# Leaving out fifteen unread products ahead of three norms in a two-model kernel

## The chip, the cores and the metric

The kernel runs on one core of one Trainium2 chip, as one launch. The metric is the device time of that launch in microseconds (us). The engines are TensorE (PE, with its weight loads shown apart as PEld), VectorE (DVE), ScalarE (ACT), GpSimd (POOL) and SyncE (SP), which issues the DMAs.

## The reference

Two small models run one after the other on a sequence of 256 tokens of width 1024, batch 1, all in float32. The first has a recurrent layer and an attention layer, each with a gated feed-forward part. The second has two hybrid layers; each projects a normed residual stream into several mixers, merges their outputs, and adds a normed result to the residual, twice:

```python
h = rmsnorm_2(h_res, n_mix_pre)
proj = jnp.einsum('bld,de->ble', h, w_in)
...
mix = jnp.einsum('bld,de->ble', merged, w_out)
h_res = h_res + rmsnorm_2(mix, n_mix_post)
f = jnp.einsum('bld,df->blf', rmsnorm_2(h_res, n_ffn_pre), w_ffn_in)
f_gate, f_up = jnp.split(f, 2, axis=-1)
f = jnp.einsum('blf,fd->bld', jax.nn.silu(f_gate) * f_up, w_ffn_out)
return h_res + rmsnorm_2(f, n_ffn_post)
```

The norm ahead of an addition to the residual (`n_mix_post`, `n_ffn_post`) needs the mean square over all 1024 features, and the next projection needs the new residual. That is the place the change touches: between `w_out` and `w_ffn_in` of both layers, and between `w_ffn_out` of layer 0 and `w_in` of layer 1.

## The kernel before

The work is a list of phases (`plan()`), and a phase is a list of weight chunks of 128 output features by up to 1024 inputs. Tokens lie along the free dimension (256, or 272 with 16 meta tokens), features along the 128 partitions. SP loads a chunk into one of eight slots; ACT rounds it to a high part, DVE subtracts to get the low part, and PE makes three products for each block of 128 inputs (`three`): high by high, high by low, low by high. Each engine has its program written out by hand in order, and engines meet at semaphores.

The three places are the starts of the phases `ffn_up2`, `a_cx1` and `ffn_up3`. The order there is:

1. The last chunk of the phase before (`mix_out0`, `ffn_down2`, `mix_out1`) ends. PE adds up the squares over the partitions with a product by a matrix of ones (`sum_up`, lines 676 and 681), into the PSUM bank `B[0]`.
2. PE runs `keep_busy(5)`: five products of ones by a piece of the parameter table, into the bank `B[3]` (line 691). No instruction reads what they write, and they wait for no semaphore.
3. ACT makes the inverse root of the sum (lines 1246 and 1247), DVE scales the first tile of the mixed output and adds it to the residual (lines 1841 and 1843), and ACT scales that tile into the high part of the next right-hand side (line 1214). The other seven tiles follow (`new_x`), with their low parts made by DVE (line 1740).
4. PE begins the phase with four chunks at once (`raw_group`), block by block: at block k it waits for the high part of tile k, makes two products for each of the four chunks (`high_two`, lines 526 and 527), waits for the low part of tile k, and makes the third product (`low_one`, line 531).

The other norms of the second kind (`ffn0`, `kv`, `ffn1`, `pre0`) have no such products. At the very end, behind the last norm, there are none either: `last_x` adds the last tiles with six useful products (lines 947 and 950).

Of the kernel before, what the change touches and what calls it, by code (L numbers as in the profile page):

```python
# [237 lines left out]
def two_layer_pair(nc, a, out):  # L238
# [4 lines left out]
    with ctx:  # L243
# [271 lines left out]
        def _(pe):  # L515
# [168 lines left out]
                last.then_inc(sum_done, 1)  # L684


            IDLE = {"ffn_up2": 5, "a_cx1": 5, "ffn_up3": 5}

            def keep_busy(n):
                for _ in range(n):  # L690
                    pe.matmul(B[3][:, 0:SEQ], ONES[:, :], PV[:, 0:SEQ], start=True, stop=True)
# [214 lines left out]
            def run(name, ready=None, beside=None, inside=None, last_turn=None):  # L906
                p = by[name]
                seen = [0, 0]
                keep_busy(IDLE.get(name, 0))
                for i, xs in enumerate(p.groups()):  # L910
# [1484 lines left out]
```

## Time and profile before

| | us |
|---|---|
| median of 3 runs | 2192.72 (2192.27 to 2192.75) |
| the profiled execution, its own time | 2192.19 |
| its span, first to last instruction | 2190.4 |
| TensorE busy in the span | 2179.9 |
| VectorE busy | 1539.2 |
| ScalarE busy | 1163.9 |
| mean granted TensorE clock | 1.000 of full speed |

An engine's busy time is the union of its instructions' times; for TensorE the ends are modelled, so that matmuls overlap in the rows and the distance of their starts says more than one row's duration. A plain float32 product appears as two matmul rows.

### The profile page before, as it was taken

The page shows a single profiled execution, that of the slowest core. Times are in us where ns is not written, and L with a number is a line of the kernel's source. Part 1 is how long each engine was busy: PE and PEld are TensorE (multiplying, and loading weights), DVE is VectorE, ACT ScalarE, POOL GpSimd, SP SyncE. Part 2 cuts the span into 40 slices and gives each one's busy share as a digit, 9 for nine tenths or more (in the row PEclk, how much of TensorE's full clock was granted, in tenths as well). Part 3 has the DMA queues.
Part 4 walks back from the last instruction along what each step waited for, and adds up shares of the span by engine and source line. Part 5 has one row for each costly group of instructions (what it writes and reads, how often), then busy time and mean ns, then how long its engine had stood idle before and what let it go on. Part 6 is the DMA issues. An engine that isn't in the chain of part 4 may idle for free.

```text
span 2190.4 us, 40748 instructions
## 1 busy us (share of the span) xinstructions
PE 2179.9 (100%) x17034; PEld 2123.9 (97%) x17034; DVE 1539.2 (70%) x2568; ACT 1163.9 (53%) x1948; POOL 2.1 (0%) x6
## 2 busy tenths in 40 slices
PE   9999999999999999999999999999999999999999
PEld 7899999999999999999999999999999999999998
DVE  7878987776577679746655765596979556667663
ACT  3644545554544667446644644454766456546443
POOL 0000000000000000000000000000000000000000
PEclk9999999999999999999999999999999999999999
DMA  8879995367655654544355555565654544455653
GB/s 348 328 256 376 391 368 211 129 237 223 183 182 170 195 170 145 163 135 145 120 168 173 159 175 168 156 200 181 199 166 145 178 127 130 155 182 175 187 177 116
DMA packets 122984, 426.75 MB, mean 195 GB/s; under 512 B 14449, under 2 KB 18993, under 8 KB 122162
## 3 DMA queue, kind: packets, MB, share of 16 engines
q1 hardware_dynamic: 122802, 424.14, 58.8%
q8 instruction: 136, 2.23, 0.4%
q14 instruction: 46, 0.38, 0.0%
HBM read 421.43 MB, written 2.66 MB: 194 GB/s over the span
## 4 chain that ended last, share of the span: by engine, by line
PE 94%; DVE 3%; ACT 2%; issue 0%; DMA 0%; ACTq 0%
PE stream L519 26%; PE stream L521 26%; PE stream L520 26%; PE stream L535 6%; PE side L741 2%; PE side L748 1%; DVE w_lo L431 1%; PE side L535 1%; PE side L670 1%; PE side L882 0%; PE stream L526 0%; PE stream L527 0%; PE stream L531 0%; PE side L531 0%; PE side L527 0%
## 5 line engine op out<-in xcount | busy, mean ns | idle before, releaser
L519 PE MATMUL stream<-h_hi,w_hi 128*128 128x272 f32 (+1 forms) x3264 | 940.6, 288 | 0.7 <-DVE h_lo L1817 0.5
L521 PE MATMUL stream<-h_hi,w_lo 128*128 128x272 f32 (+1 forms) x3264 | 931.2, 285 | 0.0
L520 PE MATMUL stream<-h_lo,w_hi 128*128 128x272 f32 (+1 forms) x3264 | 929.1, 285 | 0.0
L431 DVE TENSOR_TENSOR w_lo<-raw,w_hi 128x1024 fp32r<-128x1024 f32 (+1 forms) x640 | 766.8, 1205 | 147.4 <-ACT w_hi L1038 146.1
L1038 ACT CAST w_hi<-raw 128x1024 fp32r<-128x1024 f32 (+1 forms) x640 | 652.4, 1035 | 249.6 <-DMA raw<-in_ffn_down 87.6
L519 PEld LDWEIGHTS stream<-h_hi,w_hi 128*128 128x128 f32 x3264 | 615.5, 189 | 4.8 <-DVE h_lo L1817 1.6
L521 PEld LDWEIGHTS stream<-h_hi,w_lo 128*128 128x128 f32 x3264 | 615.7, 189 | 0.0
L520 PEld LDWEIGHTS stream<-h_lo,w_hi 128*128 128x128 f32 x3264 | 614.4, 188 | 0.5
L519 PE MATMUL stream<-f_hi,w_hi 128*128 128x256 f32 (+1 forms) x704 | 198.9, 283 | 0.0
L521 PE MATMUL stream<-f_hi,w_lo 128*128 128x256 f32 (+1 forms) x704 | 198.6, 282 | 0.0
L520 PE MATMUL stream<-f_lo,w_hi 128*128 128x256 f32 (+1 forms) x704 | 198.1, 281 | 0.0
L520 PEld LDWEIGHTS stream<-f_lo,w_hi 128*128 128x128 f32 x704 | 133.1, 189 | 0.0
L521 PEld LDWEIGHTS stream<-f_hi,w_lo 128*128 128x128 f32 x704 | 132.4, 188 | 0.0
L519 PEld LDWEIGHTS stream<-f_hi,w_hi 128*128 128x128 f32 x704 | 132.1, 188 | 0.0
L1551 DVE SCALAR_TENSOR_TENSOR mod_raw<-mod_raw,silu_c 128x1024 f32<-128x1024 f32 x96 | 116.2, 1217 | 7.5 <-DMA mod_raw<-in_mod_w 7.5
L1629 DVE TENSOR_TENSOR conv_out<-conv_in,stream 128x256 f32<-128x256 f32 (+1 forms) x88 | 37.2, 422 | 119.4 <-PE stream L521 119.4
L1146 ACT ACTIVATE conv_in<-stream 128x256 f32<-128x256 f32 (+1 forms) x104 | 40.3, 388 | 130.6 <-PE stream L521 130.6
L1758 DVE TENSOR_TENSOR conv_out<-stream,rstd 128x272 f32<-128x272 f32 (+2 forms) x104 | 44.5, 430 | 71.9 <-PE stream L521 69.1
L519 PE MATMUL stream<-y_hi,w_hi 128*128 128x256 f32 (+1 forms) x320 | 91.6, 286 | 0.0
L521 PE MATMUL stream<-y_hi,w_lo 128*128 128x256 f32 (+1 forms) x320 | 90.7, 284 | 0.0
L520 PE MATMUL stream<-y_lo,w_hi 128*128 128x256 f32 (+1 forms) x320 | 90.7, 283 | 0.0
L535 PE MATMUL stream<-h_raw,raw 128*128 128x256 f32 (+1 forms) x384 | 85.6, 380 | 0.0
(409 smaller groups left out, 3064.2 us busy)
## 6 DMA issues: line engine op xcount, KB each, us to landing
raw<-in_ffn_up SPq DMA_DIRECT2D x176, 512.0 KB, 3.6
mod_raw<-in_mod_w SPq DMA_DIRECT2D x96, 512.0 KB, 5.9
raw<-in_ffn_down SPq DMA_DIRECT2D x64, 512.0 KB, 3.7
raw<-in_a_cx SPq DMA_DIRECT2D x32, 512.0 KB, 3.9
raw<-in_up_a SPq DMA_DIRECT2D x32, 512.0 KB, 3.5
raw<-in_up_b SPq DMA_DIRECT2D x32, 512.0 KB, 3.5
raw<-in_b_kq SPq DMA_DIRECT2D x32, 512.0 KB, 3.5
raw<-in_up_c SPq DMA_DIRECT2D x32, 512.0 KB, 3.5
```

The costliest lines, as they stand in the source:

```text
L431: eng.tensor_tensor(w_lo[:, x.slot, 0:x.kb * P], raw[:, x.slot, 0:x.kb * P], w_hi[:, x.slot, 0:x.kb * P].bitcast(F32), ALU.subtract).then_ ...
L519: pe.matmul(ps, w_hi[:, x.slot, W], rhs[0][:, k, off:off + n], start=first, stop=False)
L520: pe.matmul(ps, w_hi[:, x.slot, W], rhs[1][:, k, off:off + n], start=False, stop=False)
L521: return pe.matmul(ps, w_lo[:, x.slot, W], rhs[0][:, k, off:off + n], start=False, stop=last)
L535: return pe.matmul(ps, raw[:, x.slot, wcol * P:(wcol + 1) * P], rhs[0][:, k, off:off + n], start=first, stop=last)
L670: last = pe.transpose(b[0:n, i * P:(i + 1) * P], CO[:, p.slot[t], q:q + n], ident)
L741: last = pe.matmul(b[0:m, c:c + w], key[:, at:at + m], q[:, TOK * (qt + i) + q0:TOK * (qt + i) + q0 + w], start=i == 0, stop=i == tiles - 1)
L1038: act.copy(w_hi[:, x.slot, 0:x.kb * P], raw[:, x.slot, 0:x.kb * P]).then_inc(hi_ready, 1)
L1146: act.activation(CI[:, c, 3:3 + p.T], bank[s][:, 0:p.T], func).then_inc(bank_free[s], 1)
L1551: stt(w, w, 1.0, CBC[:, :], ALU.mult, ALU.mult, accum_out=MACC[:, m:m + 1]).then_inc(mod_done, 1)
L1629: tt(dst, f, bank[s][:, 0:T], ALU.mult).then_inc(bank_free[s], 1)
L1758: tt(dst, ps, root, ALU.mult).then_inc(bank_free[s], 1)
```

## The change

The table that says how many unread products stand ahead of a phase is emptied, so that `keep_busy` issues none. Nothing else is changed: the waits, the banks, the order and the other engines' programs stay.

```diff
--- before.py
+++ after.py
@@ -684,7 +684,7 @@
                 last.then_inc(sum_done, 1)
 
 
-            IDLE = {"ffn_up2": 5, "a_cx1": 5, "ffn_up3": 5}
+            IDLE = {}
 
             def keep_busy(n):
                 for _ in range(n):
```

## Rows read from the trace of the kernel before

**Rows 1.** The page: busy time, share of the span and instructions of each engine.

```profile
PE 2179.9 (100%) x17034; PEld 2123.9 (97%) x17034; DVE 1539.2 (70%) x2568; ACT 1163.9 (53%) x1948; POOL 2.1 (0%) x6
```

**Rows 2.** The chain in order of time around the first place: start, us, piece.

```profile
1208.23 0.74 PE side L681 x2
...
1208.99 0.49 ACT rstd L1246
...
1209.51 0.44 ACT rstd L1247
...
1209.97 0.45 DVE scratch L1841
...
1210.45 0.45 DVE x_res L1843
...
1210.93 0.53 ACT h_hi L1214
...
1211.50 0.39 PE stream L526
```

**Rows 3.** TensorE's timeline at `ffn_up2`: start, us, instruction [idle before <-releaser].

```profile
1208.23 0.73 PE L681 MATMUL side<-scratch,ones 128*128 128x272 f32 x2
1208.79 2.32 PE L691 MATMUL side<-params,ones 128*128 128x256 f32 x10
1211.50 0.39 PE L526 MATMUL stream<-h_hi,w_hi 128*128 128x272 f32 x1 [0.39 <-ACT h_hi L1214]
1211.73 0.29 PE L527 MATMUL stream<-h_hi,w_lo 128*128 128x272 f32 x1
1211.86 0.29 PE L526 MATMUL stream<-h_hi,w_hi 128*128 128x272 f32 x1
```

**Rows 4.** The same at `a_cx1`.

```profile
1411.81 0.72 PE L681 MATMUL side<-scratch,ones 128*128 128x272 f32 x2
...
1415.08 0.39 PE L526 MATMUL stream<-rb_hi,w_hi 128*128 128x258 f32 x1 [0.39 <-ACT rb_hi L1214]
```

**Rows 5.** The same at `ffn_up3`.

```profile
1989.49 0.70 PE L681 MATMUL side<-scratch,ones 128*128 128x256 f32 x2
...
1992.67 0.39 PE L526 MATMUL stream<-h_hi,w_hi 128*128 128x256 f32 x1 [0.32 <-ACT h_hi L1214]
```

**Rows 6.** Line 691, all places: duration ns min/median/max, first and last start.

```profile
L691 PE MATMUL side<-params,ones x30: 379/379/379, 1208.8 to 1992.0; 128*128 128x256 f32 x30
```

**Rows 7.** TensorE's groups behind the first place (us, mean ns, idle before).

```profile
L526 PE MATMUL stream<-h_hi,w_hi 128*128 128x272 f32 x16 | 4.4, 294 | 0.4 <-ACT h_hi L1214 0.4
L526 PE MATMUL side<-h_hi,w_hi 128*128 128x272 f32 x16 | 4.3, 289 | 0.0
...
L531 PE MATMUL side<-h_lo,w_hi 128*128 128x272 f32 x16 | 3.3, 289 | 0.0
```

**Rows 8.** Weight loads at `ffn_up2`, timeline.

```profile
1211.50 0.19 PEld L526 LDWEIGHTS stream<-h_hi,w_hi 128*128 128x128 f32 x1 [0.79 <-ACT h_hi L1214]
```

**Rows 9.** Stretches at the end: PE, PEld, DVE, ACT, POOL busy, PEclk, DMA share, GB/s.

```profile
2185.00:2186.00 1.00, 0.99 (x4) 0.35 (x2) 1.00 (x4) 0.79 (x4) 0.00 (x0) 1.00 0.00 0
...
2186.10:2188.79 2.69, 0.00 (x0) 0.00 (x0) 0.36 (x2) 0.42 (x2) 0.00 (x0) 1.00 0.89 301
2188.81:2190.40 1.59, 0.00 (x0) 0.00 (x0) 0.00 (x0) 0.00 (x0) 0.00 (x0) 0.50 0.40 144
```

**Rows 10.** TensorE's timeline around its longest wait in the middle of the span.

```profile
394.10 0.28 PE L521 MATMUL stream<-h_hi,w_lo 128*128 128x256 f32 x1
395.75 0.52 PE L709 MATMUL side<-consts,a_logits 128*128 128x128 f32 x3 [1.37 <-ACT a_probs_t L1339]
```

**Rows 11.** Stretches around that wait, columns as in rows 9.

```profile
394.20:395.70 1.50, 0.18 (x2) 0.00 (x0) 0.64 (x4) 1.44 (x6) 0.00 (x0) 1.00 0.10 33
395.70:398.00 2.30, 2.25 (x16) 2.17 (x17) 1.42 (x5) 0.18 (x1) 0.00 (x0) 1.00 0.00 0
```

**Rows 12.** One line's products from 10.62 to 14.4 us (us, mean ns, idle before).

```profile
L992 PE MATMUL side<-scratch,ones 128*128 128x256 f32 x9 | 4.0, 632 | 0.0
```

**Rows 13.** The same line from 14.5 to 16.1 us.

```profile
L992 PE MATMUL side<-scratch,ones 128*128 128x256 f32 x8 | 2.1, 412 | 0.0
```

## The prediction, written before the result

> **What bounds the kernel now.** I read the page first. TensorE is busy for 2179.9 of 2190.4 us [rows 1], so a stretch in which it does less counts in full unless something else gives it back. Next I followed the chain of waits through the place where the first five products stand. There the chain leaves TensorE: the sum of squares (line 681) releases ACT, the inverse root takes two instructions, DVE scales and adds, ACT makes the first right-hand tile, and only then TensorE goes on [rows 2]. The unread products (line 691) aren't in it. The timeline of TensorE says the same from its side: the ten rows of line 691 begin at 1208.79 and are done after 2.32 us, at 1211.11, and TensorE still sits idle for 0.39 us until ACT's tile lets line 526 start at 1211.50 [rows 3]. At the second place the wait behind them is 0.39 us too, at the third 0.32 us [rows 4, 5]. So in all three places a stall of the norm lies under the products, and the products end before it does.
>
> Behind the place TensorE is the bound again: its products of the first four chunks have no idle time ahead of them but the first, 0.4 us [rows 7]. DVE and ACT, with 70% and 53% of the span [rows 1], have room, so time lost by TensorE there isn't made good by waiting less for them.
>
> **The change, part by part.** It removes 30 matmul rows of 379 ns [rows 6], ten in each place, where they cover 2.32 us each [rows 3], 6.96 us in all, with their 30 weight loads. Nothing is added or moved; no wait, DMA or bank is touched.
>
> *The products themselves: 0.* What covers them is the path from sum to tile, five instructions on ACT and DVE from 1208.97 to 1211.46 [rows 2]. It doesn't change, as it starts at line 681, which stands ahead of the products and stays. Were the cover gone, the three blocks would be worth at most 6.96 us; but the waits of 0.39, 0.39 and 0.32 us that remain behind them [rows 3 to 5] say that it is all there. A small gain could lie in line 526 starting sooner once nothing is queued ahead: its weight load (0.19 us) begins at 1211.50, after the wait [rows 8], 0.04 us after the tile is ready [rows 2]. Between 0 and 0.04 us a place, so 0.1 us over three at most. I take 0.
>
> *The stall is now bare.* Without the products TensorE does nothing from the end of line 681 to the start of line 526: 1208.96 to 1211.50, 2.54 us; 1412.53 to 1415.08, 2.55 us; 1990.19 to 1992.67, 2.48 us [rows 3 to 5]. That costs nothing by itself. What it may cost is the clock. Two idle stretches in this trace bound that. In the first, TensorE waits 1.37 us for ACT in the attention phase, and the granted clock stays at 1.00 in it and behind it [rows 10, 11]. In the second, after the last product of all, TensorE is idle from 2186.0 on; the clock is at 1.00 until 2188.8 and at 0.50 (1.2 instead of 2.4 GHz) from there [rows 9]. So 1.37 us didn't bring the lower level, and an idle stretch did within 2.8 us. The stalls of 2.5 us lie between them and much nearer to the second; whether one falls isn't shown, and I don't expect three stalls to behave alike, since they start at unrelated times and differ in the products around them.
>
> *What a fall costs.* At the start of the kernel the same product can be read at either level: line 992 takes 632 ns a row up to 14.4 us and 412 ns from 14.5 us on; nine rows fill 4.0 us at the lower level, eight fill 2.1 us at the upper [rows 12, 13]. So there TensorE ran dense, full-height products for 3.8 us (10.62 to about 14.5) before it had full speed. I take 3.8 us as the length of a low stretch. In it a product of 272 columns needs 272 columns / 1.2 GHz = 0.227 us instead of the 0.125 us between starts now (1211.73 to 1211.86, and 16 + 16 rows in the groups behind) [rows 3, 7]. The share lost is 1 - 0.125/0.227 = 0.45, so 3.8 x 0.45 = 1.7 us for one fall, three at most 5.1 us. From below a fall costs 0 if it comes so late that the clock is back before anything counts; from above, if the low stretch lasts twice as long, 3.4 us a fall and 10.2 us for three. I take 1.7 us, the only length that a row shows. Since DVE goes on at its own speed while TensorE is slow, its tiles are only earlier; nothing is lost twice.
>
> *The sum.* Two of three falls: 0 + 2 x 1.7 = +3.4 us. Against the profiled execution that is 2192.19 + 3.4 = 2195.6; the median of the runs stands 0.53 us higher, and I give the time against it: 2192.72 + 3.4 = **2196.1 us**, 0.16% slower. Two, because the stalls are nine tenths as long as the stretch that brought a fall, and nearly twice as long as the one that didn't.
>
> [...]
>
> **The rivals.**
>
> *The clock holds in all places.* For it: 1.37 us of idleness left the clock at 1.00 [rows 10, 11], and at the end 2.8 us passed before it fell [rows 9], longer than 2.55. Against it: those 2.8 us are only the time to the moment when the fall shows. Then nothing moves, the idle time of TensorE grows by about 7 us and the span by none: 2192.7 us. This one ends on the other side of the forecast, not slower; it decides as soon as no granted clock under 1.00 shows behind the three places.
>
> *All three fall, or a fall lasts longer than I take it.* For it: the three places are alike to 0.07 us in length, so what is true of one may be true of all. Against: they start at unrelated times, and the low stretch at the start of the kernel ended once the products were dense, as they are at once behind each stall [rows 7]. Time: 2192.72 + 5.1 = 2197.8 us; with stretches of double length up to 2202.9. [...]
>
> *The products delay TensorE after all.* If the modelled ends of line 691 hid a tail that holds line 526 back, leaving them out would gain. The most is the 6.96 us of their cover, 2185.8 us. Against it, the chain and the three waits name ACT's tile as the releaser, and line 526 starts 0.04 us after it [rows 2, 3]; a gain that can be measured has no place to come from. It would need line 526 to start well ahead of 2.5 us behind line 681.
>
> *The change does nothing,* because the products aren't issued: excluded, the 30 rows are in the trace [rows 6].
>
> **How the numbers follow.** A difference of about 0.2% (4.4 us) is what a measurement of this kernel can tell from no change. Chances: one or two falls (2194.4 or 2196.1) 0.47, the forecast, of which two is the likelier; no fall (2192.7) 0.23; three falls or longer ones (2197.8 and above) 0.27; a gain of more than 0.2% 0.03. The first two cases lie within 0.2% of before, so the same is 0.70, slower by more 0.27, faster by more 0.03. For eight in ten the range begins just under no fall, at 2192.3, where the lowest run of before lies, and reaches past three falls to 2199.0; what is left out is the long low stretches (about 0.08) above and a gain, or a run a little lower than before, below (about 0.1). The likeliest case alone has 2194.2 to 2196.5.
>
> **What would show it.** The chain behind line 681 should have the same five pieces, 2.5 us long, and line 526 an idle time of 2.5 instead of 0.39 us. The granted clock in stretches of a microsecond behind 1211, 1415 and 1993 us should be 0.50 for some 3 to 4 us at one or two of the places, with lines 526, 527 and 531 about 0.23 us apart there. The rest of the span should only be shifted. The prediction is wrong in its size if low stretches are longer or all three appear, wrong in its mechanism if the time rises while the clock stays at 1.00, and wrong in its premise if line 526 starts earlier behind line 681 than before.

## The result and the profile after

The median of 21 runs is 2195.71 us, against 2192.42 us for the kernel before in the same number of runs: +3.29 us, a ratio of 1.0016 with a 95% interval of 1.0010 to 1.0022. The runs of the changed kernel lie between 2193.05 and 2198.62 us, those of before between 2191.32 and 2193.28: the change has made the time larger, and less even.

The page after. TensorE is busy for 2.7 us less than in [rows 1], in a span that is 3.7 us longer (2194.1 us):

```profile
PE 2177.2 (99%) x17004; PEld 2121.8 (97%) x17004; DVE 1539.9 (70%) x2568; ACT 1164.5 (53%) x1948; POOL 2.1 (0%) x6
```

Waits of TensorE after (total, times, longest). The waits behind the unread products were 0.39, 0.39 and 0.32 us [rows 3 to 5]; now they are the whole stall:

```profile
PE stream L526 <- ACT h_hi L1214: 5.0, 2, 2.5
PE stream L526 <- ACT rb_hi L1214: 2.5, 1, 2.5
```

TensorE's timeline after, at the three places, with the sum over the partitions (676) that ends each group of four chunks:

```profile
1208.55 0.73 PE L681 MATMUL side<-scratch,ones 128*128 128x272 f32 x2
1211.82 0.59 PE L526 MATMUL stream<-h_hi,w_hi 128*128 128x272 f32 x1 [2.54 <-ACT h_hi L1214]
1212.21 0.43 PE L527 MATMUL stream<-h_hi,w_lo 128*128 128x272 f32 x1
1212.44 0.43 PE L526 MATMUL stream<-h_hi,w_hi 128*128 128x272 f32 x1
...
1225.25 0.62 PE L676 MATMUL side<-sum,ones 128*128 128x272 f32 x2
...
1413.40 0.73 PE L681 MATMUL side<-scratch,ones 128*128 128x272 f32 x2
1416.67 0.58 PE L526 MATMUL stream<-rb_hi,w_hi 128*128 128x258 f32 x1 [2.54 <-ACT rb_hi L1214]
...
1429.50 0.62 PE L676 MATMUL side<-sum,ones 128*128 128x272 f32 x2
...
1991.75 0.70 PE L681 MATMUL side<-scratch,ones 128*128 128x256 f32 x2
1994.92 0.38 PE L526 MATMUL stream<-h_hi,w_hi 128*128 128x256 f32 x1 [2.47 <-ACT h_hi L1214]
...
2007.80 0.59 PE L676 MATMUL side<-sum,ones 128*128 128x256 f32 x2
```

Line 526 starts 3.27 us behind line 681 at the first place, as it did before (1208.23 to 1211.50, [rows 3]). Behind it the products start 0.23 us apart instead of 0.13. The stretches after tell why (columns as in [rows 9], the granted clock ahead of the last two numbers):

```profile
1208.90:1211.29 2.39, 0.38 (x2) 0.00 (x0) 0.96 (x3) 0.96 (x3) 0.00 (x0) 1.00 0.80 218
1211.30:1214.70 3.40, 2.88 (x12) 2.88 (x13) 3.30 (x9) 2.60 (x7) 0.00 (x0) 0.50 0.00 1
1214.72:1226.00 11.28, 11.28 (x90) 11.20 (x90) 9.15 (x22) 5.10 (x12) 0.00 (x0) 1.00 0.01 2
...
1416.10:1419.50 3.40, 2.83 (x13) 2.83 (x14) 3.29 (x9) 2.60 (x7) 0.00 (x0) 0.50 0.06 24
...
1996.40:1999.70 3.30, 3.30 (x18) 3.30 (x17) 3.23 (x9) 2.21 (x6) 0.00 (x0) 0.50 0.00 0
```

The clock is at 0.50 for 3.4 us at each of the three places, from 0.5 and 0.6 us ahead of line 526 at the first two and from 1.4 us behind it at the third. In between it is at 1.00; at the very end it falls as in [rows 9]. The kernel before had these rows for the ends of the same groups, in its own timeline:

```profile
1223.65 0.62 PE L676 MATMUL side<-sum,ones 128*128 128x272 f32 x2
...
1426.65 0.62 PE L676 MATMUL side<-sum,ones 128*128 128x272 f32 x2
...
2004.07 0.59 PE L676 MATMUL side<-sum,ones 128*128 128x256 f32 x2
```

From line 681 to the next line 676 is the *passage* of a place, the measure used from here on. Before it took 15.42, 14.84 and 14.58 us (first rows of [rows 3 to 5]); after, 16.70, 16.10 and 16.05. That is +1.28, +1.26 and +1.47, in sum 4.0 us. The span grew by 3.7 only; the other 0.3 us lies elsewhere in the two executions.

### The profile page after: what moved, and what is told of

The parts are those of the page before. It is cut to its first block, busy times and chain, and to the rows that moved or that the text cites. A ratio compares the mean times of both kernels' runs of the same rounds, so it can differ in the third digit from the quotient of the medians.

```text
span 2194.1 us, 40688 instructions
## 1 busy us (share of the span) xinstructions
PE 2177.2 (99%) x17004; PEld 2121.8 (97%) x17004; DVE 1539.9 (70%) x2568; ACT 1164.5 (53%) x1948; POOL 2.1 (0%) x6
## 4 chain that ended last, share of the span: by engine, by line
PE 95%; DVE 2%; ACT 1%; DMA 1%; issue 0%; SPq 0%; ACTq 0%
PE stream L519 27%; PE stream L521 26%; PE stream L520 26%; PE stream L535 6%; PE side L741 2%; PE side L748 1%; DMA mod_raw_first<-in_mod_w 1%; PE side L800 1%; PE side L670 1%; PE stream L526 1%; PE side L882 0%; PE side L535 0%; PE stream L527 0%; PE stream L531 0%; PE side L531 0%
```

## The experiments

All are compared with the kernel before on the same chip in the same job. The two with a shorter stall form the first tile's high part by another rounding and let its low part take up the difference.

### One bare place at a time

```diff
-            IDLE = {"ffn_up2": 5, "a_cx1": 5, "ffn_up3": 5}
+            IDLE = {"a_cx1": 5, "ffn_up3": 5}
```

and the same with `a_cx1` or `ffn_up3` left out. The expectations:

> The five unread products are left out ahead of ffn_up2 alone; the other two places keep theirs. Theory A (the granted clock falls behind a bare stall, and the low stretch is all of the loss): the profiled execution shows 0.50 at most once, behind about 1212 us and for 3.4 us as in the changed kernel; where it does, the way from line 681 to line 676 is about 1.3 us longer than 15.4 us, and the median is +0.8 to +1.4 us over the kernel before. Theory B (the loss is not the clock's: a restart of TensorE from an empty queue, or DVE and ACT coming late, costs a third of 3.3 us at each place): +1.1 us in every run, with the clock at 1.00.

> The five unread products are left out ahead of a_cx1 alone. Theory A: 0.50 at most once, behind about 1415 us; median +0.8 to +1.4 us, spread over runs by more than 1 us, since not every execution falls. Theory B: +1.1 us in every run with the clock at 1.00. If the three places add up, the medians of the three kernels with one bare place each sum to about +3.3 us.

> The five unread products are left out ahead of ffn_up3 alone. Theory A: 0.50 at most once, behind about 1993 us; median +0.8 to +1.5 us. Theory B: +1.1 us in every run with the clock at 1.00. Sum of the three one-place kernels about +3.3 us by either.

Measured, against 2192.34 us for before: 2193.77 with `ffn_up2` bare (ratio 1.0005, 0.9996 to 1.0014), 2193.47 with `a_cx1` (1.0003, 0.9994 to 1.0012), 2194.00 with `ffn_up3` (1.0006, 0.9997 to 1.0014): +1.43, +1.13 and +1.66. The first and the last lie a little above what was expected. No interval alone excludes no change, and their sum of 4.2 agrees with 3.29 only within such widths. The profiles say more. With `ffn_up2` bare, timeline and stretches:

```profile
1209.12 0.72 PE L681 MATMUL side<-scratch,ones 128*128 128x272 f32 x2
1212.39 0.39 PE L526 MATMUL stream<-h_hi,w_hi 128*128 128x272 f32 x1 [2.55 <-ACT h_hi L1214]
...
1226.05 0.62 PE L676 MATMUL side<-sum,ones 128*128 128x272 f32 x2
...
1212.40:1213.80 1.40, 1.40 (x11) 1.40 (x12) 1.36 (x5) 1.09 (x3) 0.00 (x0) 1.00 0.00 0
1213.90:1217.20 3.30, 3.30 (x17) 3.30 (x16) 3.23 (x9) 2.15 (x6) 0.00 (x0) 0.50 0.00 0
```

Here the clock fell 1.5 us after TensorE had gone on, and the passage is 16.93 us, +1.51. With `ffn_up3` bare, timeline and stretches:

```profile
1988.95 0.70 PE L681 MATMUL side<-scratch,ones 128*128 128x256 f32 x2
1992.12 0.39 PE L526 MATMUL stream<-h_hi,w_hi 128*128 128x256 f32 x1 [2.47 <-ACT h_hi L1214]
...
2003.52 0.59 PE L676 MATMUL side<-sum,ones 128*128 128x256 f32 x2
...
1992.10:1996.00 3.90, 3.88 (x33) 3.88 (x33) 3.80 (x11) 2.72 (x7) 0.00 (x0) 1.00 0.00 0
1996.00:2004.00 8.00, 8.00 (x69) 7.95 (x68) 7.74 (x19) 4.22 (x9) 0.00 (x0) 1.00 0.01 2
```

The same bare stall, 2.47 us, and the clock holds: the passage is 14.57 us, against 14.58 before. With `a_cx1` bare it held too, behind a stall of 2.54 us, and the passage is the 14.84 us of before:

```profile
1411.92 0.73 PE L681 MATMUL side<-scratch,ones 128*128 128x272 f32 x2
1415.19 0.39 PE L526 MATMUL stream<-rb_hi,w_hi 128*128 128x258 f32 x1 [2.54 <-ACT rb_hi L1214]
...
1426.76 0.62 PE L676 MATMUL side<-sum,ones 128*128 128x272 f32 x2
...
1415.10:1419.10 4.00, 3.91 (x32) 3.92 (x33) 3.90 (x11) 2.88 (x8) 0.00 (x0) 1.00 0.03 9
```

So in these two executions neither the stall nor the empty queue costs anything, and theory B falls. In the profiles the whole loss is tied to the fall, which some executions have and others haven't. The mean clocks that come with the runs show the same split: with `a_cx1` bare, the four runs at 1.000 took 2191.76 to 2192.57 us, the six at 0.999 took 2193.44 to 2193.86, and one at 0.998 took 2194.92. Under 1.000 are 10 of 11 runs with `ffn_up2` bare and 7 of 11 with each of the others, 24 of 33, against 4 of 33 of the kernel before. The sign is a rough one: in the job of the kernels with one, two and eight products below, 7 of 26 runs of the kernel before stand at 0.999, from 2191.80 to 2193.60 us, and are no longer than its others.

### Products of one row in place of 128

```diff
-                    pe.matmul(B[3][:, 0:SEQ], ONES[:, :], PV[:, 0:SEQ], start=True, stop=True)
+                    pe.matmul(B[3][:, 0:SEQ], ONES[0:1, :], PV[0:1, 0:SEQ], start=True, stop=True)
```

> All fifteen unread products stay, with the same 256 columns and the same place, but they contract one row of the array instead of 128. Theory A1 (TensorE only has to be occupied for the clock to hold): the clock stays at 1.00 and the time is that of the kernel before, within 0.5 us. Theory A2 (the clock follows how much of the array works): TensorE is as occupied as before in the timeline, yet the clock falls behind the stalls and the time is that of the changed kernel, about +3.3 us. Theory B (an empty queue is what costs): as A1, since the queue is as full as before.

Measured: 2196.41 us against 2192.34, ratio 1.0017 (1.0008 to 1.0026), +4.07 us. Its timeline and a stretch:

```profile
1208.89 2.42 PE L691 MATMUL side<-params,ones 1*128 1x256 f32 x10
1211.51 0.39 PE L526 MATMUL stream<-h_hi,w_hi 128*128 128x272 f32 x1 [0.20 <-ACT h_hi L1214]
...
1211.90:1215.20 3.30, 3.30 (x16) 3.30 (x16) 3.23 (x9) 2.40 (x6) 0.00 (x0) 0.50 0.00 0
```

TensorE is occupied up to 0.20 us before line 526, more than in [rows 3], and yet the clock fell, at all three places of this execution, with passages 1.53, 1.53 and 1.55 us over those of before. A1 falls, and what was seen is what A2 expected: what the kernel before bought with its products is not that TensorE has instructions to run. Nor is it their number or their columns, which are the same here. Heights between 1 and 128 rows were not tried.

### One, two and eight products

The table of the kernel before with 1, 2 or 8 for each 5:

```diff
-            IDLE = {"ffn_up2": 5, "a_cx1": 5, "ffn_up3": 5}
+            IDLE = {"ffn_up2": 2, "a_cx1": 2, "ffn_up3": 2}
```

> One unread product in each place instead of five. It covers about 0.43 us, so 2.1 us of each stall are bare. Clock theory with the two lengths known so far (1.4 us never fell, 2.5 us often does): some places fall in some executions, +0.5 to +2.5 us over the kernel before, with runs spread as in the one-place kernels. If only a wholly uncovered stall fell, the time would be that of before; if anything short of full cover fell, +3.3 us.

> Two unread products in each place. They cover about 0.85 us, so 1.7 us are bare, near the 1.4 us of the attention phase that leave the clock at 1.00. Clock theory: no or few falls, 0 to +0.7 us over the kernel before, clock 1.00 behind the three places in the profiled execution. Rival (each product left out costs its share, 3.3 us / 15 = 0.22 us): 9 left out, +2.0 us in every run.

> Eight unread products in each place, three more than fit under the stall. The sixteen rows start 0.213 us apart, so line 526 can start 3.4 us behind the first of them instead of 2.7 us: +0.7 us a place, +2.1 us in all, in every run, with the clock at 1.00. This puts a price on products that do lie on the path, which the five of the kernel before would have if the third rival of the prediction were right.

Measured, against 2192.79 us: one product 2193.80 (1.0008, 0.9999 to 1.0017), two 2192.26 (0.9998, 0.9988 to 1.0007), eight 2194.45 (1.0010, 1.0001 to 1.0019). Two products are 0.53 us under before, a little outside the 0 to +0.7 expected; the interval doesn't tell it from no change. With one product, timeline and stretches at the first and the last place:

```profile
1212.74 0.54 PE L526 MATMUL stream<-h_hi,w_hi 128*128 128x272 f32 x1 [2.11 <-ACT h_hi L1214]
...
1996.23 0.39 PE L526 MATMUL stream<-h_hi,w_hi 128*128 128x256 f32 x1 [2.04 <-ACT h_hi L1214]
...
1212.90:1216.20 3.30, 3.30 (x15) 3.30 (x16) 3.23 (x10) 2.50 (x7) 0.00 (x0) 0.50 0.00 0
...
1996.20:2000.00 3.80, 3.77 (x32) 3.77 (x33) 3.70 (x11) 2.72 (x7) 0.00 (x0) 1.00 0.01 3
```

It fell at the first and second place (2.11 and 2.12 us bare) and not at the third (2.04). With two products, the first place:

```profile
1211.83 0.39 PE L526 MATMUL stream<-h_hi,w_hi 128*128 128x272 f32 x1 [1.69 <-ACT h_hi L1214]
...
1211.80:1216.00 4.20, 4.17 (x33) 4.17 (x34) 4.09 (x11) 2.82 (x7) 0.00 (x0) 1.00 0.00 0
```

1.69 us bare and no fall, here and at the other two places; the passages are 15.44, 14.85 and 14.57 us, those of before to 0.02. So, as far as this profile and these runs tell, two of the five products do all that five do, and the share-per-product rival (+2.0 us) falls. With eight, the first place:

```profile
1209.07 3.62 PE L691 MATMUL side<-params,ones 128*128 128x256 f32 x16
1212.34 0.47 PE L526 MATMUL stream<-h_hi,w_hi 128*128 128x272 f32 x1
```

Line 526 has no wait left: the products have become the path. The passages grow by 0.66, 0.64 and 0.71 us, 2.0 in sum as expected (2.1), the median by 1.66. That is what products on the path look like, and the five of before don't look so.

### A shorter stall

In the experiments the five products cost nothing and a bare stall can bring a fall, so the last pair shortens the stall. ACT makes the old part of the first tile ahead of the sum, into the place of the first right-hand tile, and DVE adds the new part there in one instruction:

```diff
+                if x.final and t == p.n - 1 and p.norm in next_raw:
+                    raw = next_raw[p.norm]
+                    act.activation(rhs_of[raw_buf[raw]][0][:, 0, p.off:p.off + p.T], X[:, 0, p.off:p.off + p.T],
+                                   ACT.Identity, scale=scale_col(raw, 0)).then_inc(old_part, 1)
...
-                    raw_high(raw, k, off, n)
+                    if k:
+                        raw_high(raw, k, off, n)
...
+                    if k == 0:
+                        dve.wait_ge(old_part, old_no[name] + 1)
+                        hi = rhs_of[raw_buf[raw]][0][:, 0, off:off + n]
+                        stt(hi, S[0], scale_col(raw, 0), hi.bitcast(F32), ALU.mult, ALU.add).then_inc(raw_hi, 1)
```

once with three products in each place and once with none.

> The stall itself is shortened: the first tile's old part (residual times weight) is made by ACT ahead of the sum, and DVE adds the new part straight into the first right-hand tile, so that the path from sum to tile has four instructions instead of five (0.44 + 0.53 us become one of about 0.5 us). Three unread products in each place. If the stall is on the path that sets the end and the clock holds, line 526 starts about 2.05 us behind line 681 instead of 2.54, and the time is 3 x 0.5 = 1.5 us under the kernel before, clock 1.00. If the stall were hidden by something else, the time would be that of before.

> The same shorter path, without any unread product, so that about 2.05 us are bare. With the lengths known (1.7 us: no fall in the profiled execution; 2.1 us: two falls; 2.5 us: three) some places fall in some executions at 1.3 to 1.5 us each: -1.5 us for the shorter stall, +1 to +3 us for falls, so -0.5 to +1.5 us against the kernel before, and slower than the covered one by at least 1 us. If the clock followed the number of products left out and not the bare length, three falls and +2.5 us.

Measured, against 2192.44 us: covered 2192.72 (1.0001, 0.9992 to 1.0010), bare 2194.27 (1.0008, 1.0000 to 1.0017). The covered one missed its gain of 1.5 us. Its timeline at the first place (lines moved: 684 is the sum, 529 and 534 are the first and third products):

```profile
1208.91 0.72 PE L684 MATMUL side<-scratch,ones 128*128 128x272 f32 x2
...
1211.68 0.40 PE L529 MATMUL stream<-h_hi,w_hi 128*128 128x272 f32 x1 [0.76 <-DVE h_hi L1854]
...
1212.68 0.29 PE L530 MATMUL side<-h_hi,w_lo 128*128 128x272 f32 x1
1213.28 0.52 PE L534 MATMUL stream<-h_lo,w_hi 128*128 128x272 f32 x2 [0.31 <-DVE h_lo L1748]
```

The first products did come 0.5 us sooner, 2.77 us behind the sum instead of 3.27. The third ones didn't: they start 4.37 us behind it, as before (4.38). The low part of that tile is made by DVE behind the second tile's two instructions, and DVE now has a third instruction for the first tile ahead of them. These are DVE's rows for that low part, in the kernel before and in the covered one:

```profile
1211.64 0.49 DVE L1740 SCALAR_TENSOR_TENSOR h_lo<-x_res,params,h_hi 128x272 fp32r<-128x272 f32 x1
...
1212.73 0.49 DVE L1748 SCALAR_TENSOR_TENSOR h_lo<-x_res,params,h_hi 128x272 fp32r<-128x272 f32 x1
```

It is done 3.9 us behind the sum before and 4.3 us here. The 0.6 us between the last two rows of TensorE, where 0.13 would do, give the gain back; the passages are 15.50, 14.97 and 14.64 us, 0.06 to 0.13 longer than before.

The bare one fell at two of the three places in its profile, with 2.05 us bare at each of those, and held at the third with 1.99. It is 1.55 us over the covered one, as expected; against the kernel before it is at +1.83 us, outside the -0.5 to +1.5 expected, since the 1.5 us of gain didn't come. Its two falls cost less than the others, 0.86 and 0.90 us of passage over the covered one: the slower products fill the wait that the covered one has ahead of its third products, and the bare one's rows have none there. No version was found that beats the kernel before.

## Why the prediction was right

**The bound, and the products at nothing.** Right. Line 526 starts as long behind line 681 as it did, and eight products show what five would have looked like on the path. The gain of 0 to 0.1 us that a free queue might have brought didn't show.

**The bare stall.** 2.54, 2.55 and 2.48 us were worked out, and 2.54, 2.54 and 2.47 are in the trace. That it costs nothing by itself was argued ahead and is now shown, by the two executions in which such a stall was bare, the clock held, and the passage stayed within 0.01 us.

**Whether the clock falls.** The two rows that bounded it, no fall behind 1.37 us and a fall within 2.8, were the right ones, and so was the expectation that the three stalls need not behave alike. The forecast of two falls is not what the profiled execution had: it had all three, the case that the second rival named. For the median it stands only by a count. With about 24 falls in 33 bare places of the one-place kernels, three places give 2.2 an execution; at 1.3 to 1.5 us each that is 2.8 to 3.3 us, and 3.29 were measured. The count is rough, since it goes by a mean clock in thousandths, which the kernel before shows at 0.999 too, without a loss.

**What a fall costs.** The term was too large: 1.7 us, and 1.26 to 1.55 us were measured (0.86 and 0.90 with the shorter stall). The slowing was right (0.125 to 0.227 us between starts). The length was not: 3.4 us instead of the 3.8 taken from line 992 at the start of the kernel, and that it came so near is luck. The 3.8 us are only the part of the slow start that line 992 fills. The view gives no granted clock under 1.00 there, so the level is read off the spacing of the products, and the products of line 963 show the lower level from the first of them on:

```profile
1.24 1.65 PE L963 MATMUL side<-ones 128*128 128x128 f32 x6 [1.24 <-DVE small L2153]
...
9.18 1.65 PE L963 MATMUL side<-ones 128*128 128x128 f32 x6
...
17.58 1.60 PE L963 MATMUL side<-ones 128*128 128x128 f32 x12
```

Six rows take the time at 1.24 and at 9.18 us that twelve take behind 14.5 us. So the slow start lasted some 13 us, and it says nothing of how long a fall lasts. With the length measured, 3.41 x 0.45 is 1.53 us, and the falls that came after TensorE had gone on cost 1.47 to 1.55. At the first two places after, the fall came 0.52 and 0.57 us before line 526 could start (1211.30 against 1211.82, 1416.10 against 1416.67), while TensorE was idle anyway: (3.41 - 0.52) x 0.45 = 1.30 against 1.28 measured, (3.41 - 0.57) x 0.45 = 1.28 against 1.26. Two falls at 1.7 and something over two at 1.4 give nearly the same sum, so part of the agreement of 2196.1 with 2195.71 is luck: one term was too large and the other too small.

**The advice on idle gaps.** The Trainium skill, page "TensorE: Matmul & The Clock Gate", section "Why this matters for your kernels", advises against idle gaps between bursts of matmuls, but only against gaps longer than the three stalls here, so taken as it stands it would not forecast a fall. The measurement differs and decides: gaps of 2.05 to 2.55 us brought the fall in some profiled executions, and gaps of 1.99 to 2.54 us left the clock at 1.00 in others.

**Left open.** Why one execution falls behind a stall and another with the same stall doesn't. The moment of the fall against the stall differs from run to run, but the rows show one thing more. Four profiled executions fell at both of the first two places, and the distance of their two falls is the same in all four, while that of their stalls is not:

| kernel | first fall, us | second fall, us | apart | starts of line 526 apart |
|---|---|---|---|---|
| the changed one | 1211.30 | 1416.10 | 204.80 | 204.85 |
| products of one row | 1211.83 | 1416.63 | 204.80 | 205.10 |
| one product | 1212.83 | 1417.63 | 204.80 | 205.12 |
| shorter stall, bare (line 529) | 1210.84 | 1415.64 | 204.80 | 204.52 |

So the stall doesn't set the moment of the fall; the falls keep a distance of their own, and the stall comes earlier or later against it. That this decides whether a stall brings a fall fits the profiles, but no run moved a stall on purpose, and it isn't shown. A few runs with one bare place took longer than one fall explains on top of the median (2194.92 with `a_cx1` bare, 2195.48 with `ffn_up3`); they were not profiled, and runs of the kernel before reach 2193.96 in that job.

## What to carry to other kernels

Before removing work that nothing reads from a full engine, look at what lies under it: if a wait is left behind it, the work is free, and it may be there for what it does to the clock. A loss that depends on the execution shows in the spread and in the mean clock before it shows in a median, and it is priced best on a short passage between two fixed instructions, where a few hundredths of a us can be told, not on 2192 us. And a shorter wait for the first operand gains only if the second one is early as well.

## What the runs showed of the hardware

With products that contract one row of the array in each place, which occupied TensorE through all but 0.20 us of the stall, the clock fell to 0.50 at all three places, and the median was 4.07 us over before, no better than with the stalls bare. With two products of full height in each place it stayed at 1.00 at all three, with 1.61 to 1.69 us bare. Each fall at the three places lasted 3.4 us, whenever it came: from 0.6 us ahead of the first product behind the stall to 1.5 us behind it. The part of it that lay under the stall cost nothing.
